# Expert rounds with raw weight slots that turn without a break, plain down products for 128 slots, and the 64-slot down product behind the gate product

## The reference, cut to what matters

```
D_MODEL = 1024; D_FF_E = 1408; N_EXP = 8; TOP_K = 2
logits = (hf @ router).astype(jnp.float32)
top_v, top_i = lax.top_k(logits, TOP_K)
wts = jax.nn.softmax(top_v, axis=-1)
gate = jnp.sum(jax.nn.one_hot(top_i, N_EXP, dtype=jnp.float32) * wts[..., None], axis=-2)
g, u = jnp.split(jnp.einsum('nd,edf->nef', hf, w_gu), 2, axis=-1)
act = jax.nn.silu(g) * u * gate[..., None].astype(h.dtype)
return jnp.einsum('nef,efd->nd', act, w_down).reshape(B, T, D)
```

## Time and profile before

| | us |
|---|---|
| median of 3 runs | 2534.3 (2526.01 to 2535.23) |
| the profiled execution: its own time | 2524.19 |
| the profiled execution: its span | 2522.5 |
| TensorE busy (matmul) | 2192.5 (87%) |
| VectorE busy | 1326.5 (53%) |
| ScalarE busy | 935.1 (37%) |
| DMA | 340.75 MB, mean 135 GB/s |

### The profile page before, as it was taken

One profiled execution on the slowest core, in us unless ns is written; L12 is line 12 of the kernel. 1 busy time (PEld: TensorE's weight loads), 2 busy tenths in 40 slices (PEclk: granted clock), 3 DMA queues, 4 the chain that ended last, 5 costly groups with the idle time before them and its releaser, 6 DMA issues. The chain is left out here.

```text
span 2522.5 us, 41799 instructions
## 1 busy us (share of the span) xinstructions
PE 2192.5 (87%) x17111; PEld 1845.0 (73%) x17111; DVE 1326.5 (53%) x1865; ACT 935.1 (37%) x1462; POOL 425.2 (17%) x459
## 2 busy tenths in 40 slices
PE   5998597999899999998994878988699898899993
PEld 4987365668899999998983665677467666787882
DVE  5566666654422222235565676644355655655546
ACT  4333024653422112114331246633344544544443
POOL 0036332541000000000064334610100000000002
PEclk8999798999899999998997899999799999999996
DMA  6331773923222232212315710021766877846645
GB/s 225 87 93 34 168 239 107 343 88 101 62 73 63 80 83 68 58 52 66 89 30 122 196 62 1 1 65 44 272 208 210 291 242 255 283 158 225 217 147 193
DMA packets 370847, 340.75 MB, mean 135 GB/s; under 512 B 90593, under 2 KB 339887, under 8 KB 369647
## 3 DMA queue, kind: packets, MB, share of 16 engines
q1 hardware_dynamic: 354447, 279.26, 36.4%
q10 hardware_dynamic: 11520, 41.95, 5.1%
q0 software_dynamic: 4704, 17.04, 1.7%
HBM read 287.42 MB, written 50.79 MB: 134 GB/s over the span
## 5 line engine op out<-in xcount | busy, mean ns | idle before, releaser
L2839 DVE TENSOR_TENSOR w_lo<-w_raw,w_hi 128x2048 fp32r<-128x2048 f32 (+1 forms) x138 | 306.5, 2228 | 156.8 <-ACT w_hi L2677 156.4
L2677 ACT CAST w_hi<-w_raw 128x2048 fp32r<-128x2048 f32 (+1 forms) x138 | 255.0, 1856 | 47.9 <-PE ps L2609 29.3
L2577 PE MATMUL ps<-w_hi,h_hi 128*128 128x512 f32 (+1 forms) x528 | 203.5, 385 | 20.6 <-DVE w_lo L2839 20.6
L2577 PE MATMUL ps<-w_hi,h_lo 128*128 128x512 f32 (+1 forms) x528 | 198.2, 375 | 0.0
L2577 PE MATMUL ps<-w_lo,h_hi 128*128 128x512 f32 (+1 forms) x528 | 198.1, 375 | 0.0
L3121 PE MATMUL ps<-ffn_h_hi,w_hi_ffn 128*128 128x320 f32 x704 | 161.5, 311 | 5.5 <-DVE ffn_h_lo L379 4.2
L3121 PE MATMUL ps<-ffn_h_lo,w_hi_ffn 128*128 128x320 f32 x704 | 161.3, 310 | 0.0
L3121 PE MATMUL ps<-ffn_h_hi,w_lo_ffn 128*128 128x320 f32 x704 | 161.3, 310 | 0.0
L1869 DVE TENSOR_REDUCE tm<-ps 128x1 f32<-128x768 f32 (+1 forms) x140 | 111.7, 818 | 49.7 <-PE ps L1765 31.6
L2577 PEld LDWEIGHTS ps<-w_hi,h_hi 128*128 128x128 f32 x528 | 100.4, 190 | 49.8 <-issue 22.6
L571 PE MATMUL ps<-w_hi_in,h_hi 128*128 128x454 f32 x320 | 122.4, 382 | 4.8 <-DVE w_lo_in L153 3.3
(11 more groups left out here) (478 smaller groups left out, 5155.1 us busy)
## 6 DMA issues: line engine op xcount, KB each, us to landing
w_raw<-in_moe_w_gu SPq DMA_DIRECT2D x186, 512.0 KB, 5.1
w_raw<-in_moe_w_down SPq DMA_DIRECT2D x41, 1024.0 KB, 7.3
G_decay<-in_ada_w ACTq DMA_DIRECT2D x54, 512.0 KB, 4.6
w_ahead<-in_ffn_w_gu SPq DMA_DIRECT2D x44, 512.0 KB, 5.3
slots_h<-tm SPq DMA_DIRECT2D x14, 1024.0 KB, 10.7
slots_y<-tm SPq DMA_DIRECT2D x13, 1024.0 KB, 11.6
w_ahead<-in_ffn_w_down SPq DMA_DIRECT2D x16, 704.0 KB, 4.7
oA<-in_ada_w ACTq DMA_DIRECT2D x20, 512.0 KB, 4.8
```

What stands on the lines that cost most here:

```text
L2577: mm = pe.matmul(ps[:, bank, 0:2 * columns(u)], x[:, k, tile * P:(tile + 1) * P], gate_up(wt, u, k), start=(k == 0 and n == 0), stop=(k == ...
L2677: act.copy(part(whi, n), raw_piece(n)).then_inc(s["w_hi"], 1)
L2839: dve.tensor_tensor(part(wlo, n), raw_piece(n), part(whi, n).bitcast(F32), ALU.subtract).then_inc(s["w_lo"], 1)
```

## The change

Four things are changed, all in `experts`.

1. **Raw slots turn without a break.** Piece n of a written-out round r has slot (17 r + n) % 6. The holder of a slot is always the piece six earlier, across rounds too. Inside the loop the numbers of a round are fixed (`loop_slot`), as before.
2. **128 rounds: plain down products.** `down` multiplies the raw float32 down piece with a plain copy of the activation (`act_plain`). The down pieces are not split, and the raw slot of a down piece is free when `dn` has counted its unit.
3. **128 rounds: gate pieces are split a unit earlier.** g(1,0) and g(1,1) are split at the round's start, and g(u+2, a) after `gate` of unit u.
4. **192 rounds: the down product of tile 1** comes right after the gate product of tile 1, waits for its own activation and its own piece, and has its own count `few_dn`, for which the release of the raw slot waits. `dn` rises after tile 0.

```diff
-        raw_slot = [n % RAW for n in range(NP)]
...
+        loop_slot = [(NP * STATIC + n) % RAW for n in range(NP)]
...
-            a_few = sb("act_few", [P, 2, 2, SMALL])
+            act_plain = sb("act_plain", [P, 2, 2, P])
...
-                   "pieces": {128: NP, 192: NP, 256: NP}, "units": {128: NU, 192: NU, 256: NU}, "rounds": {128: 1, 192: 1, 256: 1}}
+                   "pieces": {128: 2 * NU - 1, 192: NP, 256: NP}, "units": {128: NU, 192: NU, 256: NU}, "rounds": {128: 1, 192: 1, 256: 1},
+                   "few": {128: 0, 192: NU, 256: 0}}
...
+            def next_pieces(u):
+
+                return [n for n, (kind, v, _) in enumerate(ORDER) if kind == "g" and v == u + 2]
...
+            def raw_slot(r, n, ahead=0):
+
+                if isinstance(r, int) and r + ahead < STATIC:
+                    return (NP * (r + ahead) + n) % RAW
+                return loop_slot[n]
...
+            def holder(r, n, ahead):
+
+                if not ahead:
+                    return n - RAW
+                if isinstance(r, int):
+                    return NP + n - RAW
+                return max(m for m in range(NP) if loop_slot[m] == loop_slot[n])
...
             def wait_raw_free(eng, r, n):
 
-                if is_first(r) and n < 0:
+                kind, u, _ = ORDER[n]
+                if size(r) == 128 and kind == "d":
+                    eng.wait_ge(s["dn"], count("units", r, u + 1))
                     return
-                eng.wait_ge(s["w_hi"], count("pieces", r, n + 1))
-                eng.wait_ge(s["w_lo"], count("pieces", r, n + 1))
-                if isinstance(r, int) and size(r - 1 if n < 0 else r) == 192:
-                    kind, u, _ = ORDER[n % NP]
+                eng.wait_ge(s["w_hi"], rank(r, n))
+                eng.wait_ge(s["w_lo"], rank(r, n))
+                if size(r) == 192:
                     if kind == "g":
-                        eng.wait_ge(s["gu"], tile_count(r - 1 if n < 0 else r, u, 1))
+                        eng.wait_ge(s["gu"], tile_count(r, u, 1))
                     else:
-                        eng.wait_ge(s["dn"], count("units", r - 1 if n < 0 else r, u + 1))
+                        eng.wait_ge(s["few_dn"], count("few", r, u + 1))
...
                     def down(r, u, tile):
                         c = size(r)
-                        pe.wait_ge(s["a_lo"], unit_done(r, u))
-                        pe.wait_ge(s["w_lo"], count("pieces", r, at("d", u) + 1))
+                        pe.wait_ge(s["a_lo"], tile_count(r, u, tile) if few(c, tile) else unit_done(r, u))
+                        if c == 128 or few(c, tile):
+                            pe.wait_ge(s[f"raw{raw_slot(r, at("d", u))}"], landed(r, at("d", u)))
+                        else:
+                            pe.wait_ge(s["w_lo"], rank(r, at("d", u)))
...
+                            if c == 128:
+                                for half in range(2):
+                                    mm = pe.matmul(ps[:, 4 + half, :], act_plain[:, u % 2, b, :], down_rows_raw(r, u, b, half),
+                                                   start=st, stop=sp_)
                                 continue
...
                             for tile in order:
                                 multiply(r, u, tile)
+                                if u and few(c, tile):
+                                    down(r, u - 1, tile)
...
-                            if u and c == 192:
-                                down(r, u - 1, 1)
-                        for tile in range(len(order)):
+                        for tile in order:
                             down(r, NU - 1, tile)
...
+                        if c == 128:
+                            act.copy(act_plain[:, u % 2, 0:blocks_of(u)], act_turned(c, u, tile)).then_inc(s["a_lo"], 1)
+                            return
...
+                        if c == 128:
+                            split(r, at("g", 1, 0))
+                            split(r, at("g", 1, 1))
                         for u in range(NU - 1):
                             gate(r, u, order[0])
+                            if c == 128:
+                                for n in next_pieces(u):
+                                    split(r, n)
+                                take(r, u, 0)
+                                continue
                             split(r, 3 * u + 2)
```

More of the change, by code:

```diff
@@ L2276, in experts @@
             names = (self.NORM + " w_in io zeroed moved_pool mm_t lg_t mm chain diff expd chosen count turned_t h_tok slots table scattered issued "
-                     "blk_in h_turned h_hi h_lo w_hi w_lo gu silu prod a_turned a_hi a_lo dn y_act y_dve y_store y_free "
+                     "blk_in h_turned h_hi h_lo w_hi w_lo gu silu prod a_turned a_hi a_lo dn few_dn y_act y_dve y_store y_free "
                      + " ".join(f"raw{q}" for q in range(RAW)))
@@ L2574, in multiply @@
                             if k == 0 or k == 4 and u < NU - 1:
-                                pe.wait_ge(s["w_lo"], count("pieces", r, at("g", u, k // 4) + 1))
+                                pe.wait_ge(s["w_lo"], rank(r, at("g", u, k // 4 if u < NU - 1 else 0)))
                             for n, (x, wt) in enumerate(((hhi, whi), (hhi, wlo), (hlo, whi))):
@@ L2673, in split @@
                     def split(r, n, ahead=0):
[L2674 to L2675 removed]
+                        act.wait_ge(s[f"raw{raw_slot(r, n, ahead)}"], landed(r, n, ahead))
                         wait_used(act, r, hl_before[n] + NP * ahead)
[L2677 removed]
+                        act.copy(part(whi, n), raw_piece(r, n, ahead)).then_inc(s["w_hi"], 1)
                     def gate(r, u, tile):
@@ L2837, in split @@
                     def split(r, n, ahead=0):
-                        dve.wait_ge(s["w_hi"], count("pieces", r, NP * ahead + n + 1))
-                        dve.tensor_tensor(part(wlo, n), raw_piece(n), part(whi, n).bitcast(F32), ALU.subtract).then_inc(s["w_lo"], 1)
+                        dve.wait_ge(s["w_hi"], rank(r, n, ahead))
+                        dve.tensor_tensor(part(wlo, n), raw_piece(r, n, ahead), part(whi, n).bitcast(F32), ALU.subtract).then_inc(s["w_lo"], 1)
                     def gate(r, u, tile):
```

84 lines of the change are left out of this document (51 added, 33 removed).

## The result

The changed kernel takes 2497.24 us, the median of 4 runs (2494.45 to 2502.2). The kernel before, in 4 runs beside them, takes 2530.16 (2524.13 to 2535.23). The ratio is 0.9873 with the interval 0.9848 to 0.9898: 32 us faster, between 26 and 38.

A forecast was written before the change was run, and what follows sets the result against it. Bound in the 128 rounds: latency loops, TensorE waiting for late splits. R2 -9.1, R4 -7.0, R3's start -1.6, three 192 ends -3.5: -21.2 us, taking the median from 2534.3 to 2513; range 2500 to 2525.

The forecast's parts named there:

- the last step of the sum: Profiled execution to median: the profiled 2503.0 us keeps the old 10.1 us distance, so the median goes to 2513.1.
- The end wait of R2: At R2's end, TensorE would newly wait 1.3 us for the second part of the next block.
- the product of unit 0: At a 128 round's start, VectorE does two subtractions before this product, so TensorE waits longer: +1.3 us a round.
- The three ends of 192 rounds: Ends of R0, R1, R3: the moved down product hides the turn's wait, about 1.2 us each, -3.5 us in all.
- ScalarE waiting for `w_raw` and TensorE behind it: Sign that the forecast is wrong: these waits with units over 10 us would mean weight transfers bound the 128 rounds.
- The unit, taken at 9.5 us: A 128 round's unit: gate product 5.70, down product 3.45 and 0.38 us, against 8.9 us for three piece transfers.
- The clock at unit 0, "I take no loss": After 2.2 us idle at unit 0, TensorE's clock would not fall: -2.5 us in R2, -1.7 in R4.
- The raw slots, "I take 0": 128 rounds' weight pieces: the unbroken turn removes no wait itself and pays for down slots held longer; 0 us.
- part of it comes back: Rival, chance 0.20: clock still falls at unit 0, 192 ends give nothing; gain 12 to 17 us, 2519.
- the transfers: Rival, chance 0.12: weight transfers become the bound, a 128 round not shorter than its pieces; 2524 us.
- Exposed weight loads: Rival, chance 0.06: plain down products' weight loads are not hidden, 88 records cost 16.7 us; 2530 us.
- the starved queue: Rival, chance 0.04: a down piece's slot held until its product starves the queue; slower, 2550 us.

The follow-up runs named there:

- the turn alone: The kernel before with only the unbroken turn of the raw slots added; 2528.83 us, ratio 1.0003 (0.9987 to 1.002).
- the repeat: The changed kernel run once more with no edit; 2500.39 us (2495.51 to 2506.6), ratio 0.9893 to the kernel before.

## Why the prediction was right, and where it was too small

**The steps that failed.** The time came 15.8 us under the forecast. Most of it, 8.3 us, is the last step of the sum, which carried one execution's distance of 10.1 us from its median over to the new kernel; it measured 1.75 us. The other is a term that the sum of the rounds had at nothing, the drain that goes with a removed wait, some 2 us a round. The mechanism, waits for the splits that the early splits and plain products take away, came as forecast. Both are worked out below.

**Right.** The waits for `w_lo` (9.8 us a round) and `act_lo` are gone, and the kernel with late splits, which brings most of them back, loses 20.1 us. The plain product costs 0.43 us a record, as taken from the earlier trace rows. The end wait of R2 is 1.29 us (1.3 forecast), the product of unit 0 +1.46 (1.3). The three ends of 192 rounds gave 1.45, 1.06 and about 1.2 us (3.5 forecast), R3's start the clock's 1.6. "ScalarE waiting for `w_raw` and TensorE behind it" was named as what would be wrong; the first half came, the second only with 0.2 us.

**The unit, taken at 9.5 us, is 9.13.** I added 5.70 + 3.45 + 0.38. The 5.70 begins with a product that had just waited, and the 0.38 is a length that includes the drain of the last record, which the next product does not wait for: from start to start without a wait these are 5.56, 3.43 and 0.14. After a wait, though, the drain is over before the idle time begins. So a wait that goes takes about 0.4 us a unit with it beyond the number in brackets, or 2 us a round for five. This term was missing in both rounds. It is worked out from rows; no run isolates it.

**The clock at unit 0, "I take no loss", failed in part.** It fell in R2 in both traces and in R4 in one of two, at 1.6 us each time, and in seven of twelve rounds over all traces with that idle piece. With nine products in the gap it stayed. The Trainium skill says on the page "TensorE: Matmul & The Clock Gate" (Why this matters for your kernels) that idle gaps between bursts put the clock back; the 2.39 us here bear that out more than I allowed, and the 1.74 us of the earlier trace rows never did. The loss was below the 2.5 of before, so R2 still gained 0.9. After R4's two waits the clock did not fall in the trace of before, from which I read that it would not; with the same instructions it fell to 0.72 in one of two later traces (the turn alone), so that reading rests on too few. At R4's end I had kept the old wait of 1.3 us for `h_lo` whole and added 1.0; the trace shows 0.66 + 0.50, 1.1 us less.

**The raw slots, "I take 0".** As a term of the sum from before to after this held: TensorE waits 0.2 us behind the transfers in R4 and not at all in R2. What failed is the reasoning that the turn "removes no wait by itself". It was right alone (1.0003), and wrong beside the faster 128 rounds, because I tested the transfers for a steady unit only, 8.9 us against 9.5, and not for the round's first unit, which hangs on when d(0) and the pieces behind it are issued. The kernel with the old turn loses 3.8 to 5.3 us, and with half of the bytes none of TensorE's waits for `act_plain` is left. The sum never counted what the turn averts, and so is no worse for it.

**The rivals.** Of "part of it comes back" the clock came in part and the ends did not. Of "the transfers" the wait came, but in front of ScalarE, 12 to 15 us a round, and the unit was no longer for it. Exposed weight loads and the starved queue did not appear: the spacing is 0.43 us, and a unit takes 9.13 us with each down slot kept to its product.

**What it comes to.** 2513 to 2497.24 is 15.8 us. The rounds gave 24.3 us (22.8 in the repeat) and not 21.2: 3.1. The stage began 3.5 us earlier (in the repeat 0.8 later), and the rest gave 0.9. The other 8.3 us are the step from the profiled execution to the median: I kept the 10.1 us by which the old one lay below its median, and the new one lay 1.75 below. That median stood on three runs, 2534.3; later medians of the same kernel are 2526.27, 2528.49 and 2530.63 (of 13, 17 and 23 runs), only 2.1 to 6.4 us above the profiled execution. So 4 to 8 us of the 10.1 were scatter of the three runs. Most of the miss is that step and the scatter ahead of the stage; the repeat, at 2500.39, lies on the edge of the range. A range whose low end is worked out from the rounds alone is too narrow for that.

**Open.** Why 2.2 to 2.4 us of idle time cost clock in seven of twelve rounds and not in the others; why R0's start has two clocks; and what the copy of the activation ahead of the casts would give, which was not tried.

## What to carry to other kernels

Where a latency loop and a bandwidth limit lie close together, price each part of a change beside the others: undone alone here they are worth 8, 5, 13 and 20 us against the first trace, nearly twice the 24.3 that they gave together. When a loop of splits is run a unit ahead, look at what still stands behind a waiting cast on the in-order engine, and take off that path what can do without it. Keep apart, in a forecast, the sum in the stage and the run's offset from its median, and do not carry over an offset that three runs give. Before two short rounds of two traces are compared, look whether they ran at the same clock.

## What the runs showed of the hardware

- A plain float32 product of 128 rows with 512 columns takes 0.86 us, and three float32r products of the shape 0.68: 26% more on TensorE, for a cast and a subtraction (1.9 and 2.2 us a piece) less.
- 2.2 to 2.4 us of idle TensorE lowered the granted clock in seven of twelve rounds with the same instructions, to 0.57 and 0.66 in the windows of 4 and 5 us shown, at 1.6 us each in the changed kernel. In eight rounds without that idle piece it stayed at 1.00.
- The memory side carried 323 and 338 GB/s over whole 128 rounds of 57.75 and 56.65 us, and up to 401 GB/s in stretches of 5 us.
